# Six RMS norms: the sum of squares cut into a high and a low half on GpSimd and summed by two fp32r products inside the second weight unit, instead of by one float32 product before it

## The chip, the cores and the metric

The kernel runs on one core of one Trainium2 chip. The metric is the device time of one execution in microseconds (us); smaller is better.

## What is computed

The input x is 512 tokens of 1024 features, float32. Two layers of FFN, mixer and FFN are followed by a matrix-memory layer (the A layer) and an attention layer (the C layer). The blocks begin with an RMS norm, which is what the change touches:

```python
def _rmsnorm(x, gain):
    x32 = x.astype(jnp.float32)
    y = x32 * lax.rsqrt(jnp.mean(x32 * x32, axis=-1, keepdims=True) + NORM_EPS)
    return (y * gain.astype(jnp.float32)).astype(x.dtype)

for layer in range(DEPTH):
    x = x + FFN_RES_WEIGHT * _swiglu(_rmsnorm(x, ffn1_norm[layer]), ...)
    x = x + _hybrid_mixer(_rmsnorm(x, mix_norm[layer]), ...)
    x = x + FFN_RES_WEIGHT * _swiglu(_rmsnorm(x, ffn2_norm[layer]), ...)
return _rmsnorm(x, final_norm)
```

## The kernel before

The activations lie with features on the partitions: x is 8 tiles (KT = 8) of 128 features by 512 tokens. A product of full precision is made of three fp32r products, since both operands are cut into a high part (what fp32r keeps) and a low part (the rest): `pe_three` issues `h_hi*w_hi` (L419), `h_lo*w_hi` (L420) and `h_hi*w_lo` (L421). All weights come as one stream of units of 128 x 1024 numbers, four slots deep (SLOTS = 4). For each unit SP loads `w_raw`, ScalarE (ACT) writes `w_hi` (L353, `act_cut`), VectorE (DVE) writes `w_lo` over `w_raw` (L393, `dve_cut`), and TensorE (PE) waits for `lo_ready` and spends 8 x 3 = 24 products on it. There is no scheduler: each engine runs its own hand-written list, in program order, and semaphores join them.

The norm is applied late. The products start on x times gain, not yet divided by the root. Meanwhile ACT squares each tile (L361), GpSimd (POOL) adds the 8 squares into `sqsum` (`pool_squares`, L381 and L384), PE sums `sqsum` over the partitions by a product with a matrix of ones into `bank[7]` (`pe_sum_squares`, L444), ACT takes the root (`act_root`, L370) and DVE the reciprocal (`dve_norm`, L414) into `rstd`. The finished units are multiplied by `rstd` as they leave PSUM (L831 in a mixer, L772 in an FFN). There are six such norms: one each ahead of the mixer, the second FFN, the first FFN of layer 1, its mixer, its second FFN, and one ahead of the C layer. Units are counted from 0 from the norm on, so "unit 1" is the second unit that PE works on after it.

What stands around the root on DVE is set by the code. Behind an FFN, DVE cuts `dve_cut(n0 + 23)`, which is unit 1 of what follows, then `dve_norm(r)`; only behind `r == 3` does it cut unit 2 as well ahead of the reciprocal. Behind a mixer, units 0, 1 and 2 are cut ahead of it. In the C layer units 0, 1, 2 and 3 are.

```python
                dve_cut(n0 + 23)
                if r == 3:
                    dve_cut(n0 + 24)
                if r != FINAL:
                    dve_norm(r)
```

A mixer goes on with the cut of its unit 2 and then evacuates unit 0; an FFN first evacuates unit 0, whose `silu` on ACT stands ahead of the high half of unit 3, and then cuts unit 3.

Of the kernel before, what the change touches and what calls it, by code (L numbers as in the profile page):

```python
# [19 lines left out]
KT = D // P  # L20
# [23 lines left out]
F32 = mybir.dt.float32  # L44
# [3 lines left out]
ALU = mybir.AluOpType  # L48
# [27 lines left out]
NORMS = FINAL + 2  # L76
# [39 lines left out]
def build(nc, x_in, stream, cols_in, tab_in, rope_in, pos_in, out):  # L116
    with ExitStack() as ctx:
        def sem(name):
            return ctx.enter_context(nc.semaphore(name))
# [32 lines left out]
        sqsum = place("sqsum", [P, S])  # L152
        tmp = place("tmp", [P, 4, S])
        tmp_r = place("tmp_r", [P, 4, S], F32R, at=here[0] - 4 * 4 * S)
# [41 lines left out]
        ones_r = place("ones_r", [P, P], F32R, at=arena_bytes - 5 * P)  # L196
        v_feat = sqsum

        bank = [ctx.enter_context(nc.psum_tensor(f"bank{b}", [P, S], F32)) for b in range(3)]
# [6 lines left out]
        ones = tab[:, P:2 * P]  # L206
# [18 lines left out]
        unit_used = sem("unit_used")  # L225
        x_ready = sem("x_ready")
        sq_ready = sem("sq_ready")
        sq_added = sem("sq_added")
        h_half = sem("h_half")
        h_ready = sem("h_ready")  # L230
        ss_ready = sem("ss_ready")
# [98 lines left out]
        def norm_index(r):  # L330

            return r - 1 - (r > FINAL)
# [39 lines left out]
        def pool_squares(r):  # L372

            for m in range(KT):
                nc.gpsimd.wait_ge(sq_ready, 8 * norm_index(r) + m + 1)
                if m == 0:
                    if r > 1:
                        nc.gpsimd.wait_ge(ss_ready, norm_index(r))
                    if r in (2, 5):
                        nc.gpsimd.wait_ge(cum_ready, r // 3 + 1)  # L380
                    nc.gpsimd.tensor_copy(sqsum[:, :], tmp[:, 0, :]).then_inc(sq_added, 1)  # L381
                else:
                    nc.gpsimd.wait_ge(sq_added, 8 * norm_index(r) + m)
                    nc.gpsimd.tensor_tensor(sqsum[:, :], sqsum[:, :], tmp[:, m % 2, :],  # L384
                                            ALU.add).then_inc(sq_added, 1)

        def dve_cut(n, it=None):

# [50 lines left out]
        def pe_h_arrive(r):  # L439
            return lambda kt: nc.tensor.wait_ge(h_ready, KT * r + kt + 1)  # L440

        def pe_sum_squares(r):
            nc.tensor.wait_ge(sq_added, KT * norm_index(r) + KT)
            nc.tensor.matmul(bank[7][:, :], ones, sqsum[:, :], start=True, stop=True).then_inc(ss_ready, 1)  # L444

        def load(sp, n, source):
            sp.wait_ge(unit_used, n - SLOTS + 1)
# [604 lines left out]
        def _(pe):  # L1052
            def ffn(f, r, n0):
                def up(c, it, arrive=None):
                    pe.wait_ge(up_evac, count(UP_UNITS * f + c + 1, it, 4))
                    pe_unit(n0 + c, it, bank[c][:, :], h_hi, h_lo, arrive)

                up(0, None, first_arrive if r == 1 else pe_h_arrive(r - 1))
                if r > 1:
                    pe_sum_squares(r - 1)  # L1060
                for c in range(1, 4):
                    if r == 1 and c == 2:
                        pe.wait_ge(x_ready, KT)
                    up(c, None)
                    if r == 1 and c == 1:
                        lam_sums()
                        first_factors()
                with pe.Fori(1, FT // 2) as it:
                    for c in range(4):
                        up(c, it)  # L1070
                n0 += UP_UNITS

                def down(j, it, order, tile):
                    s = (n0 + j) % SLOTS
                    pe.wait_ge(lo_ready, count(n0 + j + 1, it, SLOTS))
                    pe.wait_ge(hid_ready, count(FT * f + j + 1, it, 4))
                    for m in order:
                        if j == 0 and m < 4:
                            pe.wait_ge(up_evac, UP_UNITS * (f + 1) + m + 1)
                        ins = pe_three(bank[m][:, :], w_hi[:, s, P * m:P * m + P], w_lo[:, s, P * m:P * m + P],  # L1080
                                    hid_hi[:, tile, :], hid_lo[:, tile, :], j == 0 and it is None, False)
                    ins.then_inc(unit_used, 1)

                for j in range(4):
                    down(j, None, (4, 5, 6, 7, 0, 1, 2, 3), j)
                with pe.Fori(0, 3) as it:
                    for c in range(4):
                        s = (n0 + c) % SLOTS
                        pe.wait_ge(lo_ready, count(n0 + 4 + c + 1, it, SLOTS))
                        pe.wait_ge(hid_ready, count(FT * f + 4 + c + 1, it, 4))  # L1090
                        tile = bass.ds(it * 4 + (4 + c), 1)
                        xhi = hid_hi[:, tile, :].rearrange("p o n -> p (o n)")
                        xlo = hid_lo[:, tile, :].rearrange("p o n -> p (o n)")
                        for m in range(8):
                            ins = pe_three(bank[m][:, :], w_hi[:, s, P * m:P * m + P], w_lo[:, s, P * m:P * m + P],
                                        xhi, xlo, False, False)
                        ins.then_inc(unit_used, 1)
                for j in range(16, 19):
                    down(j, None, range(8), j)

                pe.wait_ge(lo_ready, n0 + FT - 1)
                pe.wait_ge(hid_ready, FT * (f + 1))
                for m in range(8):
                    for j in range(19, 22):
                        s = (n0 + j) % SLOTS
                        if m == 0 and j == 21:
                            pe.wait_ge(lo_ready, n0 + FT)
                        ins = pe_three(bank[m][:, :], w_hi[:, s, P * m:P * m + P], w_lo[:, s, P * m:P * m + P],
                                    hid_hi[:, j, :], hid_lo[:, j, :], False, j == 21)
                        if m == 7:  # L1110
                            ins.then_inc(unit_used, 1)
                    if m < 7:
                        ins.then_inc(down_done, 1)

            def mixer(layer, r, n0):
# [128 lines left out]
                for i in range(AHEAD):  # L1244
                    for kt in range(KT):
                        if i == 0:
                            pe.wait_ge(h_ready, KT * (r - 1) + kt + 1)
                        in_step(i, kt)
                    if i == 0:
                        pe_sum_squares(r - 1)  # L1250
                    if i == 4:
                        turn_v(0)
                for k in range(NSTEP):
# [1362 lines left out]
        def _(pe):  # L2616
# [183 lines left out]
            for i, (kind, t) in enumerate(C_ORDER[:C_HEADS_AT]):  # L2800
                if i < 3:
                    pe.wait_ge(x_ready, x_count(NORMS - 1) + A_OUT_BANK.index(i) + 1)
                if kind in ("ckv", "cq"):
                    dense(kind, t, 0, KT)
                if i == 0:
                    pe_sum_squares(NORMS - 1)
                if kind == "kpe":
                    dense(kind, t, 0, KT, kv_sums)
                if (kind, t) == ("cq", 0):
# [238 lines left out]
```

## Time and profile before

| | |
|---|---|
| median of 3 runs | 2619.42 us (2616.99 to 2619.45) |
| profiled execution | 2617.52 us, of which 2615.7 us are the span of the trace |
| granted TensorE clock | 1.000 |
| PE busy | 99% of the span |
| DVE busy | 54% |
| ACT busy | 39% |
| POOL busy | 9% |

An engine's busy share says how full its list is. Durations of PE's matmuls overlap, so the distance between two starts tells what one costs, not its duration.

### The profile page before, as it was taken

The numbers are of one execution on the slowest core, as the hardware profiler recorded it, in microseconds if no ns is written. First come the engines' busy times: TensorE is split into PE (matmuls) and PEld (weight loads), VectorE is DVE, ScalarE is ACT, GpSimd is POOL, SyncE is SP. The second block draws the span as 40 slices with busy tenths as digits, with TensorE's granted clock in tenths as the row PEclk, the third lists the DMA queues.
The fourth block names the chain that finished last, engine by engine and source line by source line (L and its number), as shares of the span: only waits on it lengthen the run. The fifth ranks groups of instructions, "written<-read, shape, count | busy, mean of one in ns | idle before, by whom it ended". The sixth has DMA issues, their size and how long they took to land.

```text
span 2615.7 us, 33036 instructions
## 1 busy us (share of the span) xinstructions
PE 2600.1 (99%) x12326; PEld 2122.3 (81%) x12326; DVE 1417.8 (54%) x1863; ACT 1023.4 (39%) x1592; POOL 233.7 (9%) x172
## 2 busy tenths in 40 slices
PE   8999999999999999999999999999999999999999
PEld 7888887878888888888887778888887888888877
DVE  5444248875444335444258765444236657845773
ACT  4222135654222223222136653222235554334663
POOL 0000024201000010000034101000001110012210
PEclk9999999999999999999999999999999999999999
DMA  4222233113222223222232112222222222322221
GB/s 165 96 96 96 96 99 103 65 41 105 96 96 96 96 81 112 96 96 96 96 112 90 57 62 93 96 97 96 97 95 73 81 89 85 105 97 93 85 71 55
DMA packets 70323, 239.13 MB, mean 91 GB/s; under 512 B 8528, under 2 KB 10832, under 8 KB 70224
## 3 DMA queue, kind: packets, MB, share of 16 engines
q1 hardware_dynamic: 69792, 236.91, 26.6%
q8 instruction: 65, 1.06, 0.2%
q10 hardware_dynamic: 432, 0.87, 0.1%
q14 instruction: 34, 0.28, 0.0%
HBM read 230.15 MB, written 2.10 MB: 89 GB/s over the span
## 4 chain that ended last, share of the span: by engine, by line
PE 93%; DVE 3%; issue 2%; ACT 1%; DVEq 1%; POOL 0%; POOLq 0%; DMA 0%; ACTq 0%; SPq 0%
PE bank L419 20%; PE bank L421 20%; PE bank L420 20%; PE score L419 5%; PE score L420 5%; PE score L421 5%; PE flip_bank L419 2%; PE flip_bank L421 2%; PE flip_bank L420 2%; PE score L1182 1%; PE flip_bank L1210 1%; PE bank L2768 1%; PE score L2736 1%; PE score L1923 1%; PE bank L1232 1%
## 5 line engine op out<-in xcount | busy, mean ns | idle before, releaser
L393 DVE TENSOR_TENSOR w_lo<-w_raw,w_hi 128x1024 fp32r<-128x1024 f32 x425 | 526.2, 1240 | 538.4 <-ACT w_hi L353 527.3
L419 PE MATMUL bank<-h_hi,w_hi 128*128 128x512 f32 x1840 | 733.4, 399 | 1.1 <-DVE w_lo L393 1.1
L421 PE MATMUL bank<-h_hi,w_lo 128*128 128x512 f32 x1840 | 717.4, 390 | 0.0
L420 PE MATMUL bank<-h_lo,w_hi 128*128 128x512 f32 x1840 | 716.4, 389 | 0.0
L353 ACT ACTIVATE w_hi<-w_raw 128x1024 fp32r<-128x1024 f32 x427 | 447.5, 1051 | 383.6 <-DMA w_raw<-stream 383.0
L419 PEld LDWEIGHTS bank<-h_hi,w_hi 128*128 128x128 f32 x1840 | 345.7, 188 | 75.3 <-issue 5.0
L421 PEld LDWEIGHTS bank<-h_hi,w_lo 128*128 128x128 f32 x1840 | 345.4, 188 | 73.2
L420 PEld LDWEIGHTS bank<-h_lo,w_hi 128*128 128x128 f32 x1840 | 346.0, 188 | 70.8 <-issue 2.4
L553 ACT ACTIVATE hid_hi<-tmp 128x512 f32 (+1 forms) x88 | 55.6, 632 | 408.1 <-DVE tmp L778 408.1
L772 DVE TENSOR_TENSOR tmp<-bank,rstd 128x512 f32<-128x512 f32 x132 | 91.1, 691 | 148.3 <-PE bank L421 148.0
L548 ACT ACTIVATE tmp<-tmp 128x512 f32<-128x512 f32 x88 | 55.6, 632 | 248.7 <-DVE tmp L772 248.7
L419 PE MATMUL score<-h_hi,w_hi 128*128 128x512 f32 x384 | 149.5, 389 | 0.0
L421 PE MATMUL score<-h_hi,w_lo 128*128 128x512 f32 x384 | 149.4, 389 | 0.0
L420 PE MATMUL score<-h_lo,w_hi 128*128 128x512 f32 x384 | 149.4, 389 | 0.0
L419 PE MATMUL bank<-hid_hi,w_hi 128*128 (+1 forms) x352 | 136.9, 389 | 0.0
L420 PE MATMUL bank<-hid_lo,w_hi 128*128 (+1 forms) x352 | 136.9, 389 | 0.0
L421 PE MATMUL bank<-hid_hi,w_lo 128*128 (+1 forms) x352 | 136.9, 389 | 0.0
L381 POOL COPY sqsum<-tmp 128x512 f32<-128x512 f32 x6 | 3.7, 611 | 1215.3 <-ACT tmp L361 1215.3
L787 DVE TENSOR_TENSOR hid_lo<-tmp,hid_hi 128x512 f32 (+1 forms) x88 | 60.9, 692 | 79.7 <-ACT hid_hi L553 79.7
L619 ACT ACTIVATE probs<-score,softstat 128x128 f32<-128x128 f32 (+3 forms) x128 | 66.4, 525 | 70.1 <-DVE softstat L871 70.0
L419 PEld LDWEIGHTS score<-h_hi,w_hi 128*128 128x128 f32 x384 | 72.1, 188 | 15.0
L421 PEld LDWEIGHTS score<-h_hi,w_lo 128*128 128x128 f32 x384 | 72.1, 188 | 15.0
(535 smaller groups left out, 3832.8 us busy)
## 6 DMA issues: line engine op xcount, KB each, us to landing
w_raw<-stream SPq DMA_DIRECT2D x427, 512.0 KB, 3.2
tmp<-tmp SPq DMA_DIRECT2D x64, 64.0 KB, 2.0
x_tok<-x SPq DMA_DIRECT2D x4, 512.0 KB, 6.8
wx_raw<-stream SPq DMA_DIRECT2D x4, 512.0 KB, 4.5
out<-out_tok SPq DMA_DIRECT2D x8, 256.0 KB, 2.0
tmp<-qr SPq DMA_DIRECT2D x16, 64.0 KB, 2.6
tab_in_f<-tables SPq DMA_DIRECT2D x1, 704.0 KB, 10.4
cos_sin<-rope ACTq DMA_DIRECT2D x1, 512.0 KB, 4.9
```

Source lines behind the costliest of these rows:

```text
L353: nc.scalar.activation(w_hi[:, s, :], w_raw[:, s, :], ACT.Copy).then_inc(hi_ready, 1)
L393: nc.vector.tensor_tensor(w_lo[:, s, :], w_raw[:, s, :], w_hi[:, s, :].bitcast(F32), ALU.subtract).then_inc(lo_ready, 1)
L419: nc.tensor.matmul(dst, whi, xhi, start=start, stop=False)
L420: nc.tensor.matmul(dst, whi, xlo, start=False, stop=False)
L421: return nc.tensor.matmul(dst, wlo, xhi, start=False, stop=stop)
L548: nc.scalar.activation(tmp[:, 1, :], tmp[:, 0, :], ACT.Silu).then_inc(gate_silu, 1)
L553: nc.scalar.activation(dst, tmp[:, 3, :], ACT.Copy).then_inc(hid_half, 1)
L619: ins = nc.scalar.activation(probs[:, k % 2, c, 0:width], score[:, c, score_cols(STEPS[k][1])], ACT.Exp, bias=softstat[:, 2 * k + c, 0:1], ...
L772: nc.vector.tensor_tensor(tmp[:, 2 * (c % 2), :], bank[c][:, :], rstd[:, :], ALU.mult).then_inc(up_evac, 1)
L787: nc.vector.tensor_tensor(lo, tmp[:, 3, :], hi.bitcast(F32), ALU.subtract).then_inc(hid_ready, 1)
L1182: nc.tensor.matmul(score[:, c, score_cols(e)], q[rows, g % 2, P * e:P * e + P], kk[rows, g % 2, 0:P * (e + 1)], start=q is q_hi and kk is ...
L1210: ins = nc.tensor.transpose(flip_bank[:, at, P * kb:P * kb + P], probs[:, k % 2, c, P * kb:P * kb + P], identity)
```

## The change

GpSimd gets two instructions at the end of each of the six sums: a copy of `sqsum` into an fp32r tile (`tmp_r[:, 3]`) and a subtraction that leaves the rest (`tmp_r[:, 2]`), with a drain ahead of each. PE's float32 product is replaced by two fp32r products of `ones_r` with these tiles, and they stand in the middle of unit 1 (behind 4 of its 8 steps) and no longer between units 0 and 1.

```diff
@@ pool_squares
+            nc.gpsimd.drain()
+            nc.gpsimd.tensor_copy(tmp_r[:, 3, :], sqsum[:, :])
+            nc.gpsimd.drain()
+            nc.gpsimd.tensor_tensor(tmp_r[:, 2, :], sqsum[:, :], tmp_r[:, 3, :].bitcast(F32), ALU.subtract).then_inc(ss_in, 1)
@@ pe_sum_squares
-            nc.tensor.wait_ge(sq_added, KT * norm_index(r) + KT)
-            nc.tensor.matmul(bank[7][:, :], ones, sqsum[:, :], start=True, stop=True).then_inc(ss_ready, 1)
+            nc.tensor.wait_ge(ss_in, norm_index(r) + 1)
+            nc.tensor.matmul(bank[7][:, :], ones_r[:, :], tmp_r[:, 3, :], start=True, stop=False)
+            nc.tensor.matmul(bank[7][:, :], ones_r[:, :], tmp_r[:, 2, :], start=False, stop=True).then_inc(ss_ready, 1)
@@ ffn, on PE
+                def squares_beside(kt):
+                    if kt == KT // 2:
+                        pe_sum_squares(r - 1)
+
                 up(0, None, first_arrive if r == 1 else pe_h_arrive(r - 1))
-                if r > 1:
-                    pe_sum_squares(r - 1)
                 for c in range(1, 4):
-                    up(c, None)
+                    up(c, None, squares_beside if r > 1 and c == 1 else None)
@@ mixer, on PE
                     for kt in range(KT):
                         if i == 0:
                             pe.wait_ge(h_ready, KT * (r - 1) + kt + 1)
+                        if i == 1 and kt == KT // 2:
+                            pe_sum_squares(r - 1)
                         in_step(i, kt)
-                    if i == 0:
-                        pe_sum_squares(r - 1)
@@ the C layer, on PE
-                if kind in ("ckv", "cq"):
+                if i == 1:
+                    dense(kind, t, 0, KT // 2)
+                    pe_sum_squares(NORMS - 1)
+                    dense(kind, t, KT // 2, KT)
+                elif kind in ("ckv", "cq"):
                     dense(kind, t, 0, KT)
-                if i == 0:
-                    pe_sum_squares(NORMS - 1)
```

On PE, around the first norm (ahead of the first mixer), the program before has these rows. L419 to L421 are the three products of one step; the row that waits for `h_ready` is the last step of unit 0, the one that waits for `lo_ready` the first of unit 1.

```order
L419 MATMUL bank<-h_hi,w_hi 128x512 [waits h_ready]
L420 MATMUL bank<-h_lo,w_hi 128x512
L421 MATMUL bank<-h_hi,w_lo 128x512
L444 MATMUL bank<-sqsum,tab 128x512 [waits sq_added]
L419 MATMUL bank<-h_hi,w_hi 128x512 [waits lo_ready]
L420 MATMUL bank<-h_lo,w_hi 128x512
L421 MATMUL bank<-h_hi,w_lo 128x512
```

In the changed program, where the same three products are L423 to L425, it reads:

```order
L423 MATMUL bank<-h_hi,w_hi 128x512 [waits h_ready]
L424 MATMUL bank<-h_lo,w_hi 128x512
L425 MATMUL bank<-h_hi,w_lo 128x512
L423 MATMUL bank<-h_hi,w_hi 128x512 [waits lo_ready]
...
L425 MATMUL bank<-h_hi,w_lo 128x512
L448 MATMUL bank<-tmp_r,ones_r 128x512 [waits ss_in]
L449 MATMUL bank<-tmp_r,ones_r 128x512
L423 MATMUL bank<-h_hi,w_hi 128x512
```

The first product of unit 1 now follows unit 0 with nothing between them, and twelve products of unit 1 stand ahead of the sum.

On DVE the order at this norm is the same in both programs. L408 writes the last tiles of `h_lo`, the first L393 cuts unit 1, the second cuts unit 2, the third cuts unit 3:

```order
L408 SCALAR_TENSOR_TENSOR h_lo<-x,cols,h_hi 128x512 [waits h_half] x2
L393 TENSOR_TENSOR w_lo<-w_raw,w_hi 128x1024 [waits hi_ready]
L414 RECIPROCAL rstd<-tmp 128x512 [waits sd_ready]
L393 TENSOR_TENSOR w_lo<-w_raw,w_hi 128x1024 [waits hi_ready]
L831 SCALAR_TENSOR_TENSOR tmp<-bank,rstd 128x512 [waits unit_used]
L393 TENSOR_TENSOR w_lo<-w_raw,w_hi 128x1024 [waits hi_ready]
```

Nothing moved here: the cut of unit 2 stands behind the reciprocal, before and after.

On GpSimd the changed program has, at the same norm:

```order
L381 COPY sqsum<-tmp 128x512 [waits sq_ready]
L384 TENSOR_TENSOR sqsum<-sqsum,tmp 128x512 [waits sq_added,sq_ready] x7
L387 CAST tmp_r<-sqsum 128x512
L389 TENSOR_TENSOR tmp_r<-sqsum,tmp_r 128x512
L515 TENSOR_TENSOR tmp<-tmp,cos_sin 128x512 [waits rot_in_q,in_evac,rope_in_sem]
```

L387 and L389 are new; what follows them (L515, L510 before) belongs to the mixer.

## Rows read from the trace of the kernel before

**Rows 1.** The page: busy time, share of the span and instructions of each engine.

```profile
PE 2600.1 (99%) x12326; PEld 2122.3 (81%) x12326; DVE 1417.8 (54%) x1863; ACT 1023.4 (39%) x1592; POOL 233.7 (9%) x172
```

**Rows 2.** What PE waited for (us in total, times, longest).

```profile
PE bank L1289 <- DMA x_tok<-x: 7.3, 1, 7.3
...
PE bank L419 <- DVE w_lo L393: 1.1, 2, 0.6
```

**Rows 3.** Timeline of PE, first norm: start us, us, instruction.

```profile
377.68 0.39 PE L421 MATMUL bank<-h_hi,w_lo 128*128 128x512 f32 x1
377.91 1.02 PE L444 MATMUL bank<-sqsum,tab 128*128 128x512 f32 x2
...
379.00 0.40 PE L420 MATMUL bank<-h_lo,w_hi 128*128 128x512 f32 x1
```

**Rows 4.** Timeline of PE in the C layer: the sum of one key.

```profile
2412.29 0.39 PE L2723 MATMUL bank<-k_sq_hi,ones_r 128*128 128x512 f32 x1
2412.52 0.39 PE L2724 MATMUL bank<-tmp_r,ones_r 128*128 128x512 f32 x1
```

**Rows 5.** Timeline of GpSimd in the C layer (key squares).

```profile
2406.19 0.88 POOL L2209 CAST k_sq_hi<-tmp 128x512 fp32r<-128x512 f32 x1
2407.21 2.09 POOL L2211 TENSOR_TENSOR tmp_r<-tmp,k_sq_hi 128x512 fp32r<-128x512 f32 x1
...
2411.66 0.61 POOL L2209 CAST k_sq_hi<-tmp 128x512 fp32r<-128x512 f32 x1
```

**Rows 6.** Timeline of DVE over the same stretch.

```profile
2404.97 1.62 DVE L2431 TENSOR_TENSOR sqsum<-sqsum,tmp 128x512 f32<-128x512 f32 x1
2406.52 1.63 DVE L393 TENSOR_TENSOR w_lo<-w_raw,w_hi 128x1024 fp32r<-128x1024 f32 x1
```

**Rows 7.** Timeline of DVE, ACT and PE weight loads, first norm.

```profile
375.06 1.50 DVE L408 SCALAR_TENSOR_TENSOR h_lo<-x,cols,h_hi 128x512 fp32r<-128x512 f32 x1 [0.20 <-ACT h_hi L362]
376.49 1.21 DVE L393 TENSOR_TENSOR w_lo<-w_raw,w_hi 128x1024 fp32r<-128x1024 f32 x1
379.69 3.35 DVE L414 RECIPROCAL rstd<-tmp 128x512 f32<-128x512 f32 x1 [1.99 <-ACT tmp L370]
383.12 1.23 DVE L393 TENSOR_TENSOR w_lo<-w_raw,w_hi 128x1024 fp32r<-128x1024 f32 x1
...
378.97 0.69 ACT L370 ACTIVATE tmp<-bank,small 128x512 f32<-128x512 f32 x1 [1.49 <-PE bank L444]
...
384.40 0.19 PEld L419 LDWEIGHTS bank<-h_hi,w_hi 128*128 128x128 f32 x1 [0.40 <-DVE w_lo L393]
```

**Rows 8.** Timeline of PE at the start of unit 2, first mixer.

```profile
384.03 0.39 PE L421 MATMUL bank<-h_hi,w_lo 128*128 128x512 f32 x1
...
384.74 0.40 PE L420 MATMUL bank<-h_lo,w_hi 128*128 128x512 f32 x1
```

**Rows 9.** Timeline of GpSimd, first norm: its last sum.

```profile
374.49 1.52 POOL L384 TENSOR_TENSOR sqsum<-sqsum,tmp 128x512 f32<-128x512 f32 x1 [0.19 <-ACT tmp L361]
```

**Rows 10.** Timeline of the norm ahead of layer 1's mixer: PE, DVE.

```profile
1346.28 1.02 PE L444 MATMUL bank<-sqsum,tab 128*128 128x512 f32 x2
...
1344.91 1.21 DVE L393 TENSOR_TENSOR w_lo<-w_raw,w_hi 128x1024 fp32r<-128x1024 f32 x1
```

**Rows 11.** Timeline of the norm ahead of layer 1's first FFN.

```profile
986.34 1.02 PE L444 MATMUL bank<-sqsum,tab 128*128 128x512 f32 x2
...
985.11 1.21 DVE L393 TENSOR_TENSOR w_lo<-w_raw,w_hi 128x1024 fp32r<-128x1024 f32 x1
```

**Rows 12.** Timeline of the norm ahead of layer 0's second FFN.

```profile
626.39 1.02 PE L444 MATMUL bank<-sqsum,tab 128*128 128x512 f32 x2
...
627.45 0.69 ACT L370 ACTIVATE tmp<-bank,small 128x512 f32<-128x512 f32 x1 [2.08 <-PE bank L444]
...
633.94 1.23 DVE L393 TENSOR_TENSOR w_lo<-w_raw,w_hi 128x1024 fp32r<-128x1024 f32 x1 [1.65 <-ACT w_hi L353]
```

**Rows 13.** The core's span and mean granted TensorE clock.

```profile
core 0: 2615.7 us, clock 1.000
```

More of the change, by code:

```diff
@@ L227, in build @@
         sq_ready = sem("sq_ready")
-        sq_added = sem("sq_added")
+        sq_added, ss_in = sem("sq_added"), sem("ss_in")
         h_half = sem("h_half")
```

## The prediction

> **What bounds the kernel now.** I read the busy shares first: PE is busy 99% of the span, the other engines 54% or less [rows 1]. So a microsecond matters here only if it is taken from PE or put into it. The list of PE's waits says how much waiting is left: 7.3 us for the first input, and for weights, in the whole span, about 1.1 us [rows 2]. Any new wait is therefore paid in full, and any product taken away is gained in full. That sends me to the timeline around each of the six norms. The last product ahead of the sum starts at 377.68, the sum at 377.91, and the second product of unit 1 at 379.00 [rows 3]. Two ordinary products are 377.91 − 377.68 = 0.23 us apart; over longer undisturbed stretches it is 0.227, which I use.
>
> **The product itself.** 377.91 to 379.00 is 1.09 us and holds the sum and one ordinary product, so the float32 sum costs 1.09 − 0.227 = 0.86 us. The new pair is not in the trace at this place, but the same two operations are, in the C layer, 0.23 us apart [rows 4]: 0.45 us for two. Each norm gains 0.41 us on PE, six gain 2.5 us. The Trainium skill (FP8 and Floating Point Precision, TensorE Precision Notes) has true float32 as four passes through the array; four passes at 0.227 would be 0.91 us instead of 0.86, and the total below, by that rule, 0.2 us smaller. If the pair is dearer at its place (a switch of weights and bank inside a unit), the bound is the 0.86 of the float32 sum, and nothing is gained.
>
> **GpSimd's two instructions.** GpSimd ends its last sum at 374.49 + 1.52 = 376.01 [rows 9]. The same cast and subtraction, with drains, stand in the C layer: the cast 0.61 us undisturbed and 0.88 disturbed, the subtraction 2.09 disturbed, with 0.14 us ahead of it [rows 5]. Even disturbed, the two and their drains take 0.14 + 0.88 + 0.14 + 2.09 = 3.25 us: the halves are there at 379.26. PE wants them only after twelve products of unit 1, at 377.91 + 2.72 = 380.63 or later. So PE does not wait for GpSimd. Behind the two, GpSimd's list has the rope products, which wait for an evacuation by the new rstd, so nothing queued there is late.
>
> But GpSimd and DVE take turns. In the C layer the cast was issued at 2406.19 while DVE's two-input L2431 ran until 2406.59; it took 0.88 instead of 0.61. DVE's cut, next in line at 2406.52, took 1.63 instead of 1.21, since the cast was in its way; the subtraction then waited for the cut and took 2.09 [rows 5, 6, 7]. The first norm has this very pattern: the cast is ready at 376.01 + 0.14 = 376.15 while DVE's L408 runs until 376.56, and the cut of unit 1 is next at 376.49 [rows 7]. I take the durations of the C layer: w_lo of unit 1 lands at 376.49 + 1.63 = 378.12 and not at 377.70. Were the cast to leave DVE alone, since it has one input only, the cut would stay at 377.70, and the sum below would be 1.3 us smaller.
>
> **Unit 1 has lost its cover.** Until now 0.86 us of float32 product stood between unit 0 and unit 1. Now PE loads the first weights of unit 1 at about 377.69 (0.22 us ahead of the product's slot at 377.91). Rows 8 show how lateness turns into loss: w_lo landed at 384.35 [rows 7], PE wanted it at 384.04, and the second product of unit 2 came at 384.74 instead of 384.03 + 0.454 = 384.48, so 0.31 us late cost 0.26. With the cut at 378.12, unit 1 is 0.43 us late and costs 0.37. In layer 1's mixer the slot is 1346.28 and the cut lands at 1344.91 + 1.63 = 1346.54 against 1346.06: 0.48 late, 0.42 lost [rows 10]. Ahead of layer 1's first FFN it lands at 985.11 + 1.63 = 986.74 against 986.12: 0.62 late, 0.56 lost [rows 11]. Behind the mixers and in the C layer unit 1 was cut long before, and nothing is lost.
>
> **The root comes later, and in the mixers unit 2 waits for it.** This is the largest term. The sum moves behind twelve products (2.72 us). Before, ACT began the root 378.97 − 377.91 = 1.06 us after the sum's slot [rows 3, 7]. Now the pair starts at T + 2.72, with T the start of unit 1; the second of the pair starts 0.23 later and lasts 0.39, and ACT follows 0.04 behind: T + 3.38. In the first mixer T = 377.91 + 0.37 = 378.28, the root starts at 381.66, 2.69 us later than before. DVE's reciprocal is tied to the root, and the cut of unit 2 stands behind it in DVE's list (the order is not changed): reciprocal 379.69, cut 383.12 to 384.35, PE's weights at 384.40 [rows 7]. This chain has no slack, PE waits at its end already in the trace of before [rows 8]. So all of it shifts by 2.69 us: PE ends unit 1 at about 378.28 + 5.44 + 0.45 = 384.17 and begins unit 2 at about 387.1, an idle time of 2.9 us. PE's net loss at unit 2, everything before it included, is 2.69 us; layer 1's mixer, with 0.42 in place of 0.37, loses 2.74. What comes later in the mixer (the evacuations, the rope, the wait for k_lo) hangs on the same reciprocal or on PE and shifts along with them.
>
> **In the FFNs the same shift just fits.** Behind the mixer T = 626.39, the root starts at 629.77 instead of 627.45 [rows 12], 2.32 us later. Units 1 and 2 are cut already. The cut of unit 3 hangs on the root (rstd, the evacuation of unit 0, its silu, the high half): it ended at 633.94 + 1.23 = 635.17, which is 7.72 after the root, so now at 637.49. PE wants it at 626.39 + 0.45 + 48 × 0.227 − 0.22 = 637.5. Ahead of layer 1's first FFN the times are the same from T on. That is an edge with no slack: I take 0 lost, and 0.1 at each of three such norms if I am a little off. The later units have more room, since PE needs 5.44 us for a unit and a pair of units costs DVE and ACT less than PE. In the C layer unit 3 needs a high half and a cut (1.23 us [rows 7]) behind the root, and PE has units 1 and 2 to work through meanwhile, so nothing waits.
>
> **The sum.** Two mixers: 2.69 + 2.74 = +5.43. Layer 1's first FFN: 0.56 − 0.41 = +0.15. The two norms behind the mixers and that of the C layer: 3 × −0.41 = −1.23. Total +4.35 us. The profiled execution is 2617.52 us (span 2615.7), so 2621.9; the median of the runs shown is 1.9 us above that execution, so I forecast 2619.42 + 4.35 = 2623.8 us. The likeliest case alone holds 2621 to 2626: up to 1.3 less if the cast does not disturb DVE, 0.3 more on the three edges, and the spread of the three runs, 2.5 us. What the measurement can tell from no change is about 0.2%, 5.2 us; the forecast is 0.17%, so within it, though not by much.
>
> **Rivals.**
> *The clock falls in the two long waits* (slower). An idle time of 2.9 us in mid-stream has no precedent in this trace: the mean clock of the span is 1.000 [rows 13], and the only longer wait, 7.3 us, is the one for the first input [rows 2]. If the clock fell to 1.2 GHz, products would take twice the spacing. For a low stretch as long as the idle time itself, half of 2.9 us is lost each time: +2.9 in all, 2626.7 us; twice that if it stays low for twice as long. It decides as soon as each fall costs over 0.45 us, since only 0.9 us is left up to 0.2%. The Trainium skill (TensorE: Matmul & The Clock Gate, Why this matters for your kernels) warns of idle gaps between bursts of matmuls, and names half the clock as the price. No row here can confirm it. Chance 0.15.
> *The edges give way* (slower side). If the pair costs 0.3 us more at its place, each of the six norms loses it, and the three FFN edges and two mixers pass on the root's lateness: 0.3 × 6 plus some 0.3 × 5 is +3.3, 2627.1 us; a third of that already passes 0.2%. For it speaks that no such pair stands inside a unit in this trace; against it the smooth 0.23 of the C layer [rows 4]. Chance 0.15.
> *Only the cheaper product counts* (faster side). If the root's shift were covered, by the chain through the reciprocal being shorter or PE's start of unit 2 not hanging on it, the sum would be −2.5 + 1.35 for the lateness of unit 1 (0.37 + 0.42 + 0.56), −1.1 us, 2618.3; without that lateness −2.5, 2616.9. Against it stands PE's weight load, released by this very cut [rows 7]. A gain over 0.2% would need more than all six float32 products of 0.86 us, 5.2 us, give. Chance 0.05.
>
> **How the numbers follow.** The forecast case has 0.65. The range runs from 2619.0 (most of the third rival left out, the lower edge of the cast's turns and of the runs' spread in) to 2628.0, which takes in both slower cases at their first price. Slower by over 0.2%: 0.15 of the clock, 0.1 of the edges, 0.06 from the forecast's own spread, 0.31. Faster 0.02. Within 0.2%: 0.67.
>
> **What would show it.** In the trace after: a wait of PE for w_lo of unit 2 near 384 to 387 and again near 1352 to 1355, 2.9 us each, in place of 0.4; short waits for unit 1 at three norms; GpSimd's cast near 0.88 and DVE's cut near 1.63; the root 2.7 us later; the pair 0.23 apart; the clock at 1.00. The prediction is wrong if unit 2 does not wait, if PE waits for ss_in, or if the clock row shows less than 1.00 behind the long waits.

## The result: 7 us slower, and the profile after

The changed kernel takes 2625.03 us (median of 8 runs, 2622.29 to 2628.24) against 2617.79 us for the kernel before (8 runs, 2616.99 to 2619.68): a ratio of 1.0027, 95% interval 1.0018 to 1.0035. That is slower by about 7 us. The forecast was 2623.8 us and called the difference too small to tell from none. The time lies within 1.3 us of that, but partly by luck: the forecast started from a median of three runs, 2619.42 us, which is 1.6 us above that of eight. The difference itself was forecast as 4.35 us and is 7.2, and the interval lies clear of 1. Two single executions in the comparisons below, one of the kernel before (3730.00 us) and one of run 4 (4074.68 us), had mean clocks of 0.653 and 0.597 and are left out of the ratios.

Three views of the changed kernel answer to [rows 1, 2, 13]: the page, what PE waited for (us in total, times, longest), and the clock:

```profile
PE 2599.9 (99%) x12326; PEld 2123.1 (81%) x12326; DVE 1420.0 (54%) x1863; ACT 1023.6 (39%) x1592; POOL 252.3 (10%) x184
```

```profile
PE bank L423 <- DVE w_lo L397: 6.8, 5, 2.7
PE bank L1296 <- DMA x_tok<-x: 6.6, 1, 6.6
```

```profile
core 0: 2620.5 us, clock 0.999
```

PE's busy time is the same to 0.2 us. What grew is waiting: 1.1 us for `w_lo` before [rows 2], 6.8 us now, with a longest of 2.7 us. And the mean granted clock, 1.000 before, is 0.999. This profiled execution is the fastest of the eight (2622.29 us); the others show 0.999 or 0.998.

The first norm, timeline of the changed kernel (start us, us, instruction, idle before it and who ended it), in the order PE, GpSimd, DVE, ACT. It answers to [rows 3, 7, 8, 9]:

```profile
377.00 0.39 PE L425 MATMUL bank<-h_hi,w_lo 128*128 128x512 f32 x1
377.47 0.50 PE L423 MATMUL bank<-h_hi,w_hi 128*128 128x512 f32 x1
377.81 0.40 PE L424 MATMUL bank<-h_lo,w_hi 128*128 128x512 f32 x1
...
380.36 0.39 PE L448 MATMUL bank<-tmp_r,ones_r 128*128 128x512 f32 x1
380.59 0.39 PE L449 MATMUL bank<-tmp_r,ones_r 128*128 128x512 f32 x1
380.82 0.39 PE L423 MATMUL bank<-h_hi,w_hi 128*128 128x512 f32 x1
...
383.31 0.39 PE L425 MATMUL bank<-h_hi,w_lo 128*128 128x512 f32 x1
386.44 0.50 PE L423 MATMUL bank<-h_hi,w_hi 128*128 128x512 f32 x1 [2.75 <-DVE w_lo L397]
386.78 0.39 PE L424 MATMUL bank<-h_lo,w_hi 128*128 128x512 f32 x1
...
375.46 0.87 POOL L387 CAST tmp_r<-sqsum 128x512 fp32r<-128x512 f32 x1
376.48 2.08 POOL L389 TENSOR_TENSOR tmp_r<-sqsum,tmp_r 128x512 fp32r<-128x512 f32 x1
...
375.79 1.63 DVE L397 TENSOR_TENSOR w_lo<-w_raw,w_hi 128x1024 fp32r<-128x1024 f32 x1
381.74 3.35 DVE L418 RECIPROCAL rstd<-tmp 128x512 f32<-128x512 f32 x1 [4.33 <-ACT tmp L370]
385.17 1.23 DVE L397 TENSOR_TENSOR w_lo<-w_raw,w_hi 128x1024 fp32r<-128x1024 f32 x1
...
381.02 0.69 ACT L370 ACTIVATE tmp<-bank,small 128x512 f32<-128x512 f32 x1 [4.15 <-PE bank L449]
```

Read it down PE's rows. Unit 1 starts a little late (377.81 is 0.81 after 377.00, where 0.45 is the rule). The pair costs 380.82 − 380.36 = 0.46 us and waits for nothing. Then unit 1 is done and unit 2 stands until the cut that runs behind the reciprocal: 2.75 us of idle time.

Where did the span's 4.8 us (2620.5 − 2615.7) arise? The root (ACT L370) starts once in each norm, so it serves as a milestone. Before, for the norms that [rows 7, 12] don't show:

```profile
988.65 0.69 ACT L370 ACTIVATE tmp<-bank,small 128x512 f32<-128x512 f32 x1
1347.34 0.69 ACT L370 ACTIVATE tmp<-bank,small 128x512 f32<-128x512 f32 x1 [1.64 <-PE bank L444]
1595.43 0.69 ACT L370 ACTIVATE tmp<-bank,small 128x512 f32<-128x512 f32 x1 [2.08 <-PE bank L444]
2370.67 0.69 ACT L370 ACTIVATE tmp<-bank,small 128x512 f32<-128x512 f32 x1 [2.08 <-PE bank L444]
```

and in the changed kernel:

```profile
631.95 0.69 ACT L370 ACTIVATE tmp<-bank,small 128x512 f32<-128x512 f32 x1 [4.39 <-PE bank L449]
991.96 0.69 ACT L370 ACTIVATE tmp<-bank,small 128x512 f32<-128x512 f32 x1 [2.92 <-PE bank L449]
1351.73 0.69 ACT L370 ACTIVATE tmp<-bank,small 128x512 f32<-128x512 f32 x1 [4.41 <-PE bank L449]
1603.45 0.69 ACT L370 ACTIVATE tmp<-bank,small 128x512 f32<-128x512 f32 x1 [4.39 <-PE bank L449]
2378.25 0.69 ACT L370 ACTIVATE tmp<-bank,small 128x512 f32<-128x512 f32 x1 [4.39 <-PE bank L449]
```

Each root is later than before by its own norm's shift plus what the program had lost up to there. The own shift follows the prediction's working (start of unit 1 before, plus its lateness, plus 3.38, less the root before). Where the lateness came out other than forecast, the measured one is used: 0.49 us ahead of layer 1's first FFN (the second product of unit 1 less the last of unit 0 less two spacings, 988.78 − 987.84 − 0.454), 0.19 in layer 1's mixer (1348.53 − 1347.89 − 0.454). That gives 2.69 in the first mixer, 986.34 + 0.49 + 3.38 − 988.65 = 1.56 ahead of layer 1's first FFN, 1346.28 + 0.19 + 3.38 − 1347.34 = 2.51 in layer 1's mixer, and 2.32 in the other three. Subtracting them leaves the loss carried in:

| norm ahead of | root later by | own shift | carried in | lost from here to the next | forecast |
|---|---|---|---|---|---|
| mixer 0 | 2.05 | 2.69 | −0.64 | +2.82 | +2.69 |
| layer 0's second FFN | 4.50 | 2.32 | 2.18 | −0.43 | −0.41 |
| layer 1's first FFN | 3.31 | 1.56 | 1.75 | +0.13 | +0.15 |
| mixer 1 | 4.39 | 2.51 | 1.88 | +3.82 | +2.74 |
| layer 1's second FFN | 8.02 | 2.32 | 5.70 | −0.44 | −0.41 |
| C layer | 7.58 | 2.32 | 5.26 | −0.46 | −0.41 |

The first −0.64 is the shorter wait for the input (6.6 against 7.3 us), which is no work of the change. The one line that stands out is mixer 1. Behind its long wait, PE's rows and a window over the slow ones (from:to, length, busy time of PE, PEld, DVE, ACT, POOL, granted clock, DMA share, GB/s) read:

```profile
1357.16 0.50 PE L423 MATMUL bank<-h_hi,w_hi 128*128 128x512 f32 x1 [2.75 <-DVE w_lo L397]
1357.49 0.40 PE L424 MATMUL bank<-h_lo,w_hi 128*128 128x512 f32 x1
1357.73 0.52 PE L425 MATMUL bank<-h_hi,w_lo 128*128 128x512 f32 x1
1358.05 0.63 PE L423 MATMUL bank<-h_hi,w_hi 128*128 128x512 f32 x1
1358.47 0.63 PE L424 MATMUL bank<-h_lo,w_hi 128*128 128x512 f32 x1
...
1361.37 0.39 PE L425 MATMUL bank<-h_hi,w_lo 128*128 128x512 f32 x1
```

```profile
1358.00:1361.20 3.20, 3.20 (x9) 2.50 (x8) 1.44 (x2) 0.00 (x0) 0.00 (x0) 0.50 0.33 82
```

Three products behind the wait the spacing goes from 0.23 to 0.43 us, and the granted clock of the stretch is 0.50: PE is at 1.2 GHz, the lower of its two levels. The ten products from 1357.73 to 1361.37 have nine spacings, 3.64 us instead of 9 × 0.227 = 2.04. One fall of the clock costs 1.60 us. The first mixer's wait, as long, shows no fall in this execution.

Without the fall, mixer 1 lost 3.82 − 1.60 = 2.22 us, 0.5 less than forecast. Of that, 0.23 is unit 1, less late than assumed. The rest lies beside the mixer's softmax, where a product of PE (L1163, at 1387.23 in the kernel before) starts 0.06 us behind the end of the DVE instruction that it needs. One of DVE's products ahead of that ran beside a rope product of GpSimd before, and no longer does, since the rope comes later. Before and after:

```profile
1376.27 0.93 DVE L883 TENSOR_SCALAR probs<-probs,softstat,lam 128x128 f32<-128x128 f32 x1
1382.28 0.47 DVE L888 TENSOR_SCALAR probs<-probs,softstat,lam 128x128 f32<-128x128 f32 x1
```

DVE wins back 0.46 us, and PE's lag behind the program before, taken at the same product in both traces, goes from 6.0 to 5.6 us at that place (and to 5.7 by the end of the mixer).

Without the fall and the shorter input wait, the six norms lose 4.8 + 0.64 − 1.60 = 3.8 us, where the forecast had 4.35.

### The profile page after: what moved, and what is told of

Same layout as the page of the kernel before. It is cut to its first block, busy times and chain, and to the rows that moved or that the text cites. A ratio compares the mean times of both kernels' runs of the same rounds, so it can differ in the third digit from the quotient of the medians.

```text
span 2620.5 us, 33060 instructions
## 1 busy us (share of the span) xinstructions
PE 2599.9 (99%) x12326; PEld 2123.1 (81%) x12326; DVE 1420.0 (54%) x1863; ACT 1023.6 (39%) x1592; POOL 252.3 (10%) x184
## 3 DMA queue, kind: packets, MB, share of 16 engines
q8 instruction: 65, 1.06, 0.2%
## 4 chain that ended last, share of the span: by engine, by line
PE 91%; DVE 4%; issue 2%; ACT 1%; DVEq 1%; POOL 1%; DMA 0%; POOLq 0%; ACTq 0%; SPq 0%
PE bank L423 20%; PE bank L425 20%; PE bank L424 20%; PE score L423 5%; PE score L425 5%; PE score L424 5%; PE flip_bank L423 2%; PE flip_bank L424 2%; PE flip_bank L425 2%; PE score L1189 1%; PE flip_bank L1217 1%; PE bank L2775 1%; PE score L2743 1%; DVE h_lo L412 1%; PE score L1930 1%
## 5 line engine op out<-in xcount | busy, mean ns | idle before, releaser
L423 PE MATMUL bank<-h_hi,w_hi 128*128 128x512 f32 x1840 | 732.3, 398 | 6.9 <-DVE w_lo L397 6.8
L425 PE MATMUL bank<-h_hi,w_lo 128*128 128x512 f32 x1840 | 718.2, 390 | 0.0
L423 PEld LDWEIGHTS bank<-h_hi,w_hi 128*128 128x128 f32 x1840 | 346.1, 188 | 80.7 <-DVE w_lo L397 7.2
L425 PEld LDWEIGHTS bank<-h_hi,w_lo 128*128 128x128 f32 x1840 | 345.8, 188 | 73.4
L423 PE MATMUL score<-h_hi,w_hi 128*128 128x512 f32 x384 | 149.5, 389 | 0.0
L425 PE MATMUL score<-h_hi,w_lo 128*128 128x512 f32 x384 | 149.5, 389 | 0.0
L425 PE MATMUL bank<-hid_hi,w_lo 128*128 (+1 forms) x352 | 137.0, 389 | 0.0
L423 PE MATMUL bank<-hid_hi,w_hi 128*128 (+1 forms) x352 | 137.0, 389 | 0.0
L423 PEld LDWEIGHTS score<-h_hi,w_hi 128*128 128x128 f32 x384 | 72.0, 188 | 15.2
L424 PEld LDWEIGHTS score<-h_lo,w_hi 128*128 128x128 f32 x384 | 72.2, 188 | 15.0
```

The costliest lines, as they stand in the source:

```text
L423: nc.tensor.matmul(dst, whi, xhi, start=start, stop=False)
L424: nc.tensor.matmul(dst, whi, xlo, start=False, stop=False)
L425: return nc.tensor.matmul(dst, wlo, xhi, start=False, stop=stop)
```

## Experiments

Each is the changed kernel with the edit shown, unless it says otherwise. "Before" is always the kernel before, run on the same chip beside it. Since the profile of after already showed the clock, the runs are read with the mean clock that each gave.

**1. The mixers as before.** The norms ahead of the two mixers get the float32 product back at its old place and no halves on GpSimd:

```diff
 # sums on GpSimd
+if r in (1, 4):
+    return
 # pe_sum_squares
+if r in (1, 4):
+    nc.tensor.wait_ge(sq_added, KT * norm_index(r) + KT)
+    nc.tensor.matmul(bank[7][:, :], ones, sqsum[:, :], start=True, stop=True).then_inc(ss_ready, 1)
+    return
...
 # mixer
-if i == 1 and kt == KT // 2:
-    pe_sum_squares(r - 1)
 in_step(i, kt)
+...
+if i == 0:
+    pe_sum_squares(r - 1)
```

> The two norms ahead of the mixers keep the float32 product between units 0 and 1 and get no halves; the other four norms are as in the changed kernel. If the loss sits in the mixers (unit 2 waits for the root, and the clock falls behind that wait), it is gone: +0.15 (layer 1's first FFN) and 3 x -0.41 give -1.1 us against before, 2616.7, no wait of PE over 0.7 us in mid-stream, clock 1.000. If instead the pair or GpSimd's two instructions cost time at every norm, about two thirds of the +7.2 us stay: +4.8, 2622.6.

Measured: 2616.76 us (11 runs) against 2618.49, ratio 0.9995 (0.9986 to 1.0004). So all of the loss lies in the mixers. The four other norms give some 1.7 us (forecast 1.1), though the interval holds no change too. The clock is 1.000 in seven of the eleven runs.

**2. The cut of unit 2 ahead of the reciprocal.** ACT and DVE cut it at the end of the FFN, one unit earlier:

```diff
-if r == 3:
+if r in (1, 3, 4):
     dve_cut(n0 + 24)
 ...
 for i in range(AHEAD):
-    dve_cut(n0 + i + 2)
+    if i:
+        dve_cut(n0 + i + 2)
```

> As the changed kernel, but ahead of the mixers ACT and DVE cut unit 2 before the root and the reciprocal. If the order root, reciprocal, cut of unit 2 is what costs, both waits of 2.7 us go, the clock stays at 1.000, and with 1.35 us of lateness of unit 1 and 6 x -0.41 the sum is -1.1 us against before: 2616.7. If the evacuations and the rope, which still come 2 us later, were what PE really waits for, the wait turns up at the scores of the mixer and the time stays 2 to 5 us above before. Before, the first key is ready 5 us ahead of its scores, so I expect the former.

Measured: 2618.73 us (11 runs) against 2618.49, ratio 1.0001 (0.9992 to 1.0010), clock 1.000 in nine of eleven runs. The long waits are gone, and a new one has come:

```profile
PE bank L423 <- DVE w_lo L397: 1.8, 4, 0.6
...
PE flip_bank L1218 <- DVE pt_lo L902: 1.3, 2, 1.0
```

So PE stood at the reciprocal's cut, not at the reciprocal. The missing 1.3 us was looked for in layer 1's mixer, on DVE and GpSimd:

```profile
1378.43 1.23 DVE L892 SCALAR_TENSOR_TENSOR probs<-probs,softstat 128x128 f32<-128x128 f32 x1
...
1378.21 1.30 POOL L516 TENSOR_TENSOR tmp<-tmp,cos_sin 128x512 f32<-128x512 f32 x1
```

A softmax product of DVE takes 1.23 us beside GpSimd's rope product; in the kernel before the same product takes 0.35, with the rope product over by then:

```profile
1377.29 0.35 DVE L886 SCALAR_TENSOR_TENSOR probs<-probs,softstat 128x128 f32<-128x128 f32 x1
```

The root, still 2.6 us late with PE's own lag taken off, moves GpSimd's rope products onto DVE's softmax. This product and the one ahead of it (1.11 for 0.93) take 1.06 us longer together, and PE's lag behind the kernel before, product by product, grows from 0.95 to 2.02 us at its next wait for `pt_lo`. So in this profile 1.07 us of the missing 1.3 arise there, and 0.27 at a wait for `w_lo` at 1364.59. What the mixer costs without the collision was not run.

**3 and 4. The place of the pair.** In 3 the pair stands behind eighteen products of unit 1 in the mixers, in 4 behind six in all six norms:

```diff
-if i == 1 and kt == KT // 2:
+if i == 1 and kt == 6:      # run 3, mixers alone
+if i == 1 and kt == 2:      # run 4, FFNs and C layer likewise
     pe_sum_squares(r - 1)
```

> In the mixers the pair stands behind 6 of the 8 steps of unit 1, not 4: the root comes 1.36 us later. Chain alone: two mixers x 1.36 = +2.7 us against the changed kernel. Both waits grow from 2.7 to 4.1 us. If a wait of that kind lowers the clock, it now falls behind both of them in every run, 1.6 us each or more, and the fall in the changed kernel (one of two waits in its profile) is a matter of chance: at least +2.7 + 1.6 = +4.3 against its profiled run, 2626.6 or more. If the clock has nothing to do with the length of the wait, falls stay as rare as before and the median is 2625.0 + 2.7 = 2627.7 with a clock of 0.998 to 0.999.

Measured: 2627.23 us (5 runs) against 2618.49, ratio 1.0038 (1.0024 to 1.0052). All five runs have a clock under 1.000, and in the profile a fall stands behind each of the two waits. The first wait, and what follows it:

```profile
388.02 0.50 PE L423 MATMUL bank<-h_hi,w_hi 128*128 128x512 f32 x1 [4.11 <-DVE w_lo L397]
388.36 0.40 PE L424 MATMUL bank<-h_lo,w_hi 128*128 128x512 f32 x1
...
388.82 0.63 PE L423 MATMUL bank<-h_hi,w_hi 128*128 128x512 f32 x1
389.25 0.63 PE L424 MATMUL bank<-h_lo,w_hi 128*128 128x512 f32 x1
```

> At all six norms the pair stands behind 2 of the 8 steps: the root comes 1.36 us earlier than in the changed kernel, the halves are just there (0.4 us to spare by my reckoning). Chain: 2 x -1.36 = -2.7 us, the waits are 1.3 us each, and the clock holds: against before +3.9 - 2.7 = +1.2, 2619.0, clock 1.000, and a narrow spread as before. If the loss were the pair's, the halves' or the clock's at random, the median stays near 2625.

Measured: 2620.73 us (10 runs) against 2618.49, ratio 1.0006 (0.9997 to 1.0016). The longest wait is 1.4 us, no product behind it is slow, and the clock is 1.000 in seven of the ten runs:

```profile
PE bank L423 <- DVE w_lo L397: 4.1, 5, 1.4
```

So six products of place are 1.4 us of wait per mixer, as the chain has it: 1.4, 2.7 and 4.1 us at steps 2, 4 and 6.

**5. GpSimd's halves behind the cut of unit 1.** GpSimd waits for the cut, so that the cast no longer disturbs it:

```diff
+if r in (1, 3, 4):
+    nc.gpsimd.wait_ge(lo_ready, {1: FFN_UNITS, 3: LAYER_UNITS, 4: LAYER_UNITS + FFN_UNITS}[r] + 2)
 nc.gpsimd.drain()
```

> As the changed kernel, but at the three norms behind an FFN GpSimd waits with the cast until DVE has cut unit 1. The cut should take 1.21 us again instead of 1.63, unit 1 be 0.42 us earlier, and everything behind it: 3 x -0.42 = -1.3 us against the changed kernel, with the two long waits still there. If the turns of the two engines do not matter, no difference.

Measured: 2625.64 us (11 runs) against 2618.61, ratio 1.0022 (1.0013 to 1.0031). DVE's cut of unit 1 takes 1.22 us again at all three norms, but the gain on the median is not to be told from none. The eleven runs are worth more when they are sorted by clock: two at 1.000 (mean 2620.3), three at 0.999 (2623.6), five at 0.998 (2626.2), one at 0.997 (2627.4). With the same code, the time follows the clock over 7 us. In the two runs with no fall the kernel is 1.7 us over before.

**6. Only the move.** The float32 product in one piece, at the new place, and no halves:

```diff
-nc.gpsimd.drain()
-nc.gpsimd.tensor_copy(tmp_r[:, 3, :], sqsum[:, :])
...
-nc.tensor.wait_ge(ss_in, norm_index(r) + 1)
-nc.tensor.matmul(bank[7][:, :], ones_r[:, :], tmp_r[:, 3, :], start=True, stop=False)
-nc.tensor.matmul(bank[7][:, :], ones_r[:, :], tmp_r[:, 2, :], start=False, stop=True).then_inc(ss_ready, 1)
+nc.tensor.wait_ge(sq_added, KT * norm_index(r) + KT)
+nc.tensor.matmul(bank[7][:, :], ones, sqsum[:, :], start=True, stop=True).then_inc(ss_ready, 1)
```

> Only the move: the float32 product stands in the middle of unit 1, GpSimd makes no halves. The root starts at T + 2.72 + 1.06, with T at its old slot: +2.72 in each mixer, +0.15 ahead of layer 1's first FFN, 0 at the others: +5.6 us against before without a fall of the clock, with the same idle times of 2.7 to 2.9 us, so falls of 1.6 us are as likely as in the changed kernel: 2623 to 2627. If the move is harmless and the halves cost, it is at 2617.8 like before.

Measured: 2625.17 us (9 runs, 2624.17 to 2626.46) against 2618.61, ratio 1.0026 (1.0016 to 1.0035), clock 0.999 in every run. So the move alone is enough to lose 7 us. That it costs just what the whole change costs is partly chance: its chain was forecast at +5.6 us against 4.35, and its clock is never at 0.998. The profile has a fall behind the first long wait and none behind the second. The fall is longer here, products 0.43 us apart from 388.26 to 393.81, and the first product behind the wait is already slow:

```profile
387.67 0.79 PE L419 MATMUL bank<-h_hi,w_hi 128*128 128x512 f32 x1 [2.70 <-DVE w_lo L393]
388.26 0.63 PE L420 MATMUL bank<-h_lo,w_hi 128*128 128x512 f32 x1
...
393.81 0.41 PE L421 MATMUL bank<-h_hi,w_lo 128*128 128x512 f32 x1
```

That is 13 spacings in 5.55 us where 2.95 would do, and 0.59 us from the first product to the second where 0.34 is the rule behind such a wait: 2.85 us for one fall.

**7. Only the halves.** The pair at the old place of the float32 product, ahead of unit 1 (edit to the mixer; the FFN and the C layer likewise):

```diff
-if i == 1 and kt == KT // 2:
-    pe_sum_squares(r - 1)
 in_step(i, kt)
+...
+if i == 0:
+    pe_sum_squares(r - 1)
```

> Only the split: halves and pair, but between units 0 and 1 as before. PE then waits for the subtraction, 1.4 us (mixers), 1.6 (layer 1's first FFN), 0.8 at the other three, and gains 0.41 at each. Root 1.04 us later in the mixers, so +1.04 each; +1.2; 3 x +0.4: +4.5 us, 2622.3, and no wait long enough for the clock, which stays at 1.000. If the split is harmless, -2.5, 2615.3.

Measured: 2623.45 us (11 runs) against 2618.61, ratio 1.0019 (1.0010 to 1.0028), clock 1.000 in nine runs. The loss arises where PE waits for GpSimd's subtraction, at all six norms:

```profile
PE bank L448 <- POOL tmp_r L389: 5.3, 6, 1.3
```

**8. The cut first and the halves behind it** (edits 2 and 5 together).

> The two remedies together: unit 2 of the mixers cut ahead of the root, the cast behind the cut of unit 1. Left are 6 x -0.41 and 0.05, 0.06 and 0.2 us of lateness at the three norms behind an FFN, since the float32 product no longer covers unit 1: -2.2 us against before, 2615.6, clock 1.000. If the gain of the cheaper product is not real, 2617.8.

Measured: 2617.81 us (11 runs) against 2618.61, ratio 0.9998 (0.9989 to 1.0007). Again part of the expected gain is missing, and again PE waits up to 0.9 us for `pt_lo` (its lag behind the kernel before grows by 1.0 us there), and 0.8 us for `w_lo` at 1364.70 (0.6 us of lag).

**9. The best of both.** Mixers as before (1), the cut of unit 2 ahead (2), and GpSimd's halves behind the cut ahead of layer 1's first FFN (5, that norm alone).

> The mixers keep the float32 product at its old place, without halves, and unit 2 is cut ahead of the reciprocal there, which takes the 0.26 us wait that was there before the change; the other four norms have the pair inside unit 1, and ahead of layer 1's first FFN the cast waits for the cut of unit 1. 2 x -0.26, -0.41 + 0.15, 3 x -0.41: -2.0 us against before, 2616.5, clock 1.000. If cutting unit 2 first delays the rope and brings GpSimd's rope products onto DVE's softmax, as with the run that had the cut first in the changed kernel, half or more of it is lost in layer 1's mixer.

Measured: 2616.20 us (11 runs) against 2618.21, ratio 0.9992 (0.9983 to 1.0001), clock 1.000 in eight runs. This is the best version by its median, 2 us below before, but the interval still holds no change.

**10. Is it the idle time that lowers the clock?** Twelve products whose results are thrown away are put in front of the last products of unit 1 in the mixers, to fill the wait with work:

```diff
+if i == 1 and kt == KT - 1:
+    for _ in range(12):
+        nc.tensor.matmul(bank[3][:, :], ones_r[:, :], tmp_r[:, 3, :], start=True, stop=True)
```

> As the changed kernel, but in the mixers TensorE issues 12 more fp32r products of 0.227 us (their results are thrown away) ahead of the last step of unit 1, so that it works through the 2.7 us in which it otherwise waits for unit 2. The chain through the root is the same, and unit 2 begins at the same time. If the idle time itself lowers the clock, the falls behind unit 2 vanish: clock 1.000, about 2621 to 2622 us with a narrow spread, 2 to 4 us below the changed kernel. If the falls have another cause, nothing changes: 2625.

Measured: 2625.09 us (11 runs) against 2618.21, ratio 1.0025 (1.0016 to 1.0034). The clock went the way expected: six runs at 1.000, five at 0.999, none at 0.998, and no slow products in the profile. The time did not: the six runs at 1.000 have a mean of 2624.6, not 2621 to 2622. By the roots, the first mixer loses 2.69 us, as forecast for a wait without a fall. But 2.4 us more are lost ahead of layer 1's mixer, and the second mixer loses 3.6. The first of these can be followed. PE there waits for `h_lo`:

```profile
1348.06 0.50 PE L423 MATMUL bank<-h_hi,w_hi 128*128 128x512 f32 x1 [0.48 <-DVE h_lo L412]
...
1332.79 1.06 ACT L353 ACTIVATE w_hi<-w_raw 128x1024 fp32r<-128x1024 f32 x1 [6.85 <-DMA w_raw<-stream]
1333.88 1.23 DVE L397 TENSOR_TENSOR w_lo<-w_raw,w_hi 128x1024 fp32r<-128x1024 f32 x1 [6.69 <-ACT w_hi L353]
```

In the changed kernel the same unit's high half comes 3.1 us earlier, after the usual idle time of some 4.3:

```profile
1329.67 1.06 ACT L353 ACTIVATE w_hi<-w_raw 128x1024 fp32r<-128x1024 f32 x1 [4.33 <-DMA w_raw<-stream]
```

One transfer of weights landed some 2.5 us late. PE did not need that unit yet, but its cut stands ahead of the residual and the norm in DVE's list, and so `h_lo` came late for PE. Whether the filler has to do with it, and whether the ten other runs show it too, is not known: the other profiles looked at (3, 5, 6, 9 and the repetition below) have idle times of 4.2 to 4.5 us there. So the run shows that work in place of the idle time keeps the clock up more often: 6 of 11 runs against 0 of 17. The falls did not all vanish, since five runs of eleven are below 1.000. What the idle time costs without a fall can be read product by product: at unit 2 PE's lag behind the kernel before grows by 2.8 us in both mixers of this profile, as forecast for the chain alone. The excess over 2622 us lies elsewhere, some 2.2 us ahead of layer 1's mixer and 0.8 us later inside it.

**11. The changed kernel again**, on the chip of 9 and 10.

> The changed kernel itself, on the same chip as the two beside it: 2625 us, clock 0.998 to 0.999, two waits of 2.7 us.

Measured: 2625.77 us (9 runs) against 2618.21, ratio 1.0028 (1.0018 to 1.0038). Falls stand behind both long waits in this profile, and a third is in the C layer.

## Why the prediction was right about the chain and left the clock out of its sum

**The product itself**: right. The pair costs 0.46 us against 0.45, and neither waits nor lags at its place. *The edges give way* is refuted: the rows 0.23 apart ahead of, in and behind the pair refute its premise, and the three norms with no lateness of unit 1 (two second FFNs, the C layer) gained 0.43 to 0.46 us each, a little more than the 0.41 forecast.

**GpSimd's two instructions**: right. The cast took 0.87, the subtraction 2.08, the cut 1.63 (forecast 0.88, 2.09, 1.63), and the halves were there at 378.56, 1.8 us before PE came to them.

**Unit 1 has lost its cover**: right in kind. By the second product of unit 1, the first norm lost 0.36 us (forecast 0.37); ahead of layer 1's first FFN 0.49 (0.56); in layer 1's mixer 0.19 (0.42).

**The root comes later, and in the mixers unit 2 waits for it**: right. Idle times of 2.75 us twice (forecast 2.9), at the place named. Even the size is right: the profile counts from the end of the last product, the forecast from the slot of the next one, and 386.44 − 383.31 − 0.227 = 2.90. Runs 3 and 4 move the wait by 1.4 us for six products, and run 2 takes it away.

**In the FFNs the same shift just fits**: right. Of the five waits for `w_lo` in the list, two are the mixers', one the start of unit 1 ahead of layer 1's first FFN, and two, 1.1 us in all, stand past 1700 us, outside every norm, where before has them too. None is at unit 3.

**The sum**: this is the step that fell short. Its terms, which came to 4.35 us, came out at 3.8; but it has no term for the clock. 7.2 less 3.8 leaves 3.4 us, about what two falls of 1.6 us cost. The prediction gave the clock to a rival with a chance of 0.15, and by its own list of signs (the clock below 1.00 behind the long waits) its mechanism was incomplete. The call "too small to tell" (within 0.2%) fell with it: the change costs 0.27%, for which it had given a chance of 0.31. The reason given for the 0.15 was that "an idle time of 2.9 us in mid-stream has no precedent in this trace". That is no evidence against a fall, only the lack of any; and the price from which it decides, 0.45 us each, was low. *The clock falls in the two long waits* is what happened, in nearly every run. Of the 17 runs of the changed kernel (8 and 9) none has a mean clock of 1.000; of the kernel before, run beside them, 22 of 25 have in the last comparison. The nine runs at 0.999 have a mean of 2624.2 us, the eight at 0.998 one of 2626.8. Continued by the same 2.6 us to 1.000, this gives a rough estimate of 2621.6, within 0.5 us of 2617.8 + 4.35 = 2622.1. It is rough because the printed clock is coarse: 0.999 stands for one fall in the profile of after and for two in that of run 3, 0.998 for three in that of run 11. The rival's price, 1.45 us each, was near too: 1.60 for the fall in the profile, though run 6 has one of 2.85. The Trainium skill (TensorE: Matmul & The Clock Gate, Why this matters for your kernels), cited in the prediction, warns of gaps between bursts of matmuls. This case agrees, with a granted clock of 0.50 and products 0.43 us apart in place of 0.227 behind a 2.75 us wait.

What shows that the waits lower the clock, and nothing else of the change? The longest wait was varied with all other work nearly the same (each run beside the kernel before on its own chip, where that has 1.000 in 22 of 25, 26 of 31 and 21 of 26 runs):

| run | longest wait of PE for w_lo | runs with clock 1.000 | ratio |
|---|---|---|---|
| 2, cut ahead | 0.6 | 9 of 11 | 1.0001 |
| 4, pair at 2 | 1.4 | 7 of 10 | 1.0006 |
| changed | 2.7 | 0 of 17 | 1.0027, 1.0028 |
| 6, only the move | 2.7 | 0 of 9 | 1.0026 |
| 5, halves behind | 2.7 | 2 of 11 | 1.0022 |
| 3, pair at 6 | 4.1 | 0 of 5 | 1.0038 |

Run 7, with the same GpSimd and PE instructions but waits of at most 1.3 us, has 9 of 11 at 1.000. Runs 1, 8 and 9, with waits of at most 0.8 us for `w_lo`, have 7, 10 and 8 of 11. And run 10 fills the waits with work and has 6 of 11. The kernel before has some runs at 0.999 as well, and the profile of run 1 a fall in the C layer, 55 us behind the norm there and with none of the long waits in the program; every version has some runs below 1.000.

**Only the cheaper product counts**: refuted in the mixers, where the root's shift was not covered. Run 1 has only the norms where it was: forecast −1.1 us (the same figure as this rival's, but from four norms), measured −1.7, with no change inside the interval.

**Left open.** Why the first mixer's wait of 2.75 us in the profiled execution had no fall and the second's had one. Why a transfer was late in run 10's profile, and whether it was in its other runs. Whether runs 2 and 8 would show their full gain if the rope kept clear of the softmax.

## What to carry to other kernels

Moving a small product into the stream saves its own few tenths of a microsecond, but everything that hangs on its result moves by the length of what it was moved past: follow that chain (here root, reciprocal, the cut queued behind it) to the first engine that waits. When a change opens a wait of PE longer than any that the trace holds in mid-stream, price the clock's fall as part of the sum, and not as a rival, and sort repeated runs by their mean clock before reading a median. An instruction that nobody waits for can still hold back the ones queued behind it: a cut of weights ahead of the residual passed on a late transfer that PE itself would not have noticed.

## What the runs showed of the hardware that was not expected

- Where the slow products begin differs from wait to wait. In the profile of after and behind the first wait of run 3, PE first runs two or three products at full speed, and only then at 0.43 us spacing; behind the second wait of run 5 it runs six; in run 6, and behind the second wait of run 3, the first product is slow already. The slow products span 3.6 us in the profile of after, 6.1 in run 6 (387.67 to 393.81) and 3.4 in run 3 (388.82 to 392.23), although that wait is the longest of the three. With the longest wait every run had a fall, but not a longer one.
- A wait of 2.7 us does not always bring a fall: in the profiles of after and of run 6 one of two did, in run 11 both. Two of the eleven runs of 5 had none.
- A 128x128 product of DVE (0.35 us) took 1.23 us beside a two-input GpSimd instruction of 1.30. Where the two take turns, a short instruction of DVE can take over three times as long.
